# Queries and keys of heads 1 to 3 in seven block products instead of eight half-blocks

## The reference, cut to what matters

```python
def _odd_mixer(h, w_in, w_out, gammas):
    proj = h @ w_in                       # h: 512 x 1024, w_in: 1024 x 6144
    q, k, v, g = jnp.split(proj, [D_MODEL, 2 * D_MODEL, 4 * D_MODEL], axis=-1)
    o = _retention(_split_heads(q, RET_HEADS), _split_heads(k, RET_HEADS),
                   _split_heads(v, RET_HEADS), gammas)
    ...
    y = (jax.nn.silu(g.astype(jnp.float32)) * o).astype(h.dtype)
    return y @ w_out
```

## Time and profile before

| | us |
|---|---|
| median of three runs | 1286.79 (1286.78 to 1287.39) |
| the profiled execution, device time | 1287.36 |
| its span in the trace | 1285.6 |
| `r_qk(1)`, PE, from 664.75 | 21.8 |
| `r_qk(2)`, PE, from 777.24 | 21.8 |
| `r_qk(3)`, PE, from 847.99 | 21.8 |

### The profile page before, as it was taken

The page is one execution under the profiler, slowest core; times in us unless marked ns, Lnnn a source line. Parts: engine busy times, 40 slices in busy tenths (PEclk is TensorE's granted clock), DMA queues, the critical chain, the costliest instruction groups (busy, mean ns, idle before and its releaser), DMA issues.

```text
span 1285.6 us, 18945 instructions
## 1 busy us (share of the span) xinstructions
PE 1276.6 (99%) x7390; PEld 1119.9 (87%) x7390; DVE 913.6 (71%) x1171; ACT 733.5 (57%) x992; POOL 211.7 (16%) x253
## 2 busy tenths in 40 slices
PE   9999999999999999999999999999999999999998
PEld 6788888899898998989888888888889899898996
DVE  6466457578958669598754694656799876959678
ACT  6555455358557475576645552636667746457564
POOL 3121000022112211111211021111212221111211
PEclk9999999999999999999999999999999999999999
DMA  7322231469898988993854686755598899898983
GB/s 259 91 66 58 74 91 58 136 151 234 224 227 180 224 226 214 231 224 117 175 178 89 188 204 172 195 132 112 143 236 201 198 231 230 209 237 183 219 217 107
DMA packets 100409, 223.20 MB, mean 174 GB/s; under 512 B 8784, under 2 KB 25432, under 8 KB 100320
## 3 DMA queue, kind: packets, MB, share of 16 engines
q0 software_dynamic: 26912, 97.55, 39.7%
q1 hardware_dynamic: 73104, 124.11, 29.1%
q10 hardware_dynamic: 304, 0.33, 0.1%
HBM read 127.57 MB, written 2.11 MB: 101 GB/s over the span
## 4 chain that ended last, share of the span: by engine, by line
PE 90%; DVE 5%; DMA 2%; issue 1%; ACT 1%; POOL 0%; SPq 0%; POOLq 0%; DVEq 0%; ACTq 0%
PE bank L806 21%; PE bank L838 21%; PE bank L1207 12%; PE bank L1019 9%; PE bank L1124 7%; PE bank L1275 5%; PE bank L959 3%; PE bank L936 3%; PE bank L1221 2%; PE bank L986 2%; DVE w L1978 2%; PE bank L921 1%; PE bank L1173 1%; PE bank L903 1%; PE bank L901 1%
## 5 line engine op out<-in xcount | busy, mean ns | idle before, releaser
L1978 DVE TENSOR_TENSOR w<-raw_tiles,w 128x1024 fp32r<-128x1024 f32 x324 | 385.5, 1220 | 116.7 <-ACT w L1408 116.4
L1408 ACT ACTIVATE w<-raw_tiles 128x1024 fp32r<-128x1024 f32 x324 | 327.7, 1051 | 153.7 <-PE bank L838 53.7
L806 PE MATMUL bank<-h_ops,w 128*128 128x256 f32 x2688 | 325.0, 283 | 0.1
L806 PEld LDWEIGHTS bank<-h_ops,w 128*128 128x128 f32 x2688 | 323.9, 192 | 1.0 <-DVE h_ops L2210 0.3
L838 PE MATMUL bank<-w,arena_q 128*128 128x512 f32 x1332 | 305.1, 390 | 0.1
L838 PEld LDWEIGHTS bank<-w,arena_q 128*128 128x128 f32 x1332 | 249.1, 188 | 52.9 <-DVE x L2254 1.7
L2741 POOL DMA_DIRECT2D raw_tiles<-raw_tiles x176 | 152.6, 902 | 664.9 <-DVE w L1978 439.3
L1207 PE MATMUL bank<-w,h_ops 128*128 128x512 f32 x672 | 154.1, 390 | 0.0
L1207 PEld LDWEIGHTS bank<-w,h_ops 128*128 128x128 f32 x672 | 125.7, 188 | 25.7
L1124 PE MATMUL bank<-h_ops,w 128*128 128x512 f32 (+1 forms) x480 | 89.5, 347 | 0.0
L1124 PEld LDWEIGHTS bank<-h_ops,w 128*128 128x128 f32 x480 | 77.3, 189 | 11.4 <-DVE h_ops L1963 0.2
(11 more groups left out here) (190 smaller groups left out, 1425.4 us busy)
## 6 DMA issues: line engine op xcount, KB each, us to landing
raw_tiles<-raw_tiles POOLq DMA_DIRECT2D x176, 512.0 KB, 5.6
raw_tiles<-in_ffn_w_in SPq DMA_DIRECT2D x64, 512.0 KB, 5.7
raw_tiles<-in_ffn_w_out SPq DMA_DIRECT2D x64, 512.0 KB, 6.2
raw_tiles<-in_odd_w_in SPq DMA_DIRECT2D x32, 512.0 KB, 4.7
raw_tiles<-in_even_w_in SPq DMA_DIRECT2D x48, 256.0 KB, 3.2
raw_tiles<-in_odd_w_in SPq DMA_DIRECT2D x32, 256.0 KB, 5.2
raw_tiles<-in_odd_w_out SPq DMA_DIRECT2D x16, 512.0 KB, 6.1
x<-in_x SPq DMA_DIRECT2D x8, 512.0 KB, 5.7
```

Of the source, the lines that this page charges most:

```text
L806: mm = pe.matmul(bank[first + b][:, 256 * m:256 * m + 256], w_slots[use_slot(use)][:, p, k, c:c + P], h_ops[:, H_BLOCK[op], q, k, :], star ...
L1408: nc.scalar.activation(w_flat(use_slot(use), 0, half), raws[tile][:, 1024 * half:1024 * half + 1024], ACT.Copy).then_inc(m_hi, 1)
L1978: nc.vector.tensor_tensor(w_flat(use_slot(use), 1, half), raws[use_tile(key)][:, 1024 * half:1024 * half + 1024], w_flat(use_slot(use), 0, ...
```

## The change

`r_qk(h)` for h = 1, 2, 3 becomes a seven-product scheme over 2x2 blocks of 256 token columns and 256 output columns (queries are the first column block of the weights, keys the second). Head 0 stays as it is. Each product is 2 output groups x 4 contraction tiles x 3 passes = 24 matmuls of 128x256, 168 in all instead of 96 of 128x512. The A operands are those which the vg section uses already.

```diff
+QK_ORDER = ((A11, B11, "X"), (A12, B21, "Z"), (S1, T1, "Y"), (S2, T2, "X"), (S4, B22, "Y"), (S3, T3, "X"), (A22, T4, "X"))
...
             def r_qk(h):
...
+                for i, (op, value, to) in enumerate(QK_ORDER):
+                    use = USE["qk", h, i // 2]
+                    for m in range(2):
...
+                        elif i == 3:
+                            pe.wait_ge(qk_copied[0], 2 * (h - 1) + m + 1)
+                        elif i == 4:
+                            pe.wait_ge(qk_copied[1], h)
+                        elif i == 5:
+                            pe.wait_ge(qk_copied[2], 2 * (h - 1) + m + 1)
+                        else:
+                            pe.wait_ge(qk_summed, 4 * (h - 1) + 3 + m)
+                        if m == 0:
+                            pe.wait_ge(m_lo, split_count("qk", h, value, 1))
```

A weight value is 128x4x256 and two values share a slot: B11 and B21, T1 and T2, B22 and T3, T4 alone. The weight tile of 128x2048 holds query and key columns side by side, so T1 is one half of a tile's columns added to the other, in pieces of 256 columns:

```diff
+            def add_columns(n, value, half, dst, src):
...
+                pool.dma_start(to, of, accum_op=ALU.add).then_inc(t_made[value][half], 16)
...
             for h in range(RH):
...
                 if h % 2 == 0:
+                    for value in (T1, T3, T2, T4):
+                        qk_weight_sum(h + 1, value)
                     gn_inv_std(h)
                     continue
...
+                    for value in (T1, T3, T2, T4):
+                        qk_weight_sum(2, value)
```

More of the change, by code:

```diff
@@ L184, in a_slot, with product_done, split_count, qk_source @@
     return (7 * g + i) % A_SLOTS
+def product_done(key, t=1):
+    return 2 * PRODUCT_COUNT[key] + t + 1
 def use_done(use, t=1):
-    return 2 * PRODUCT_COUNT[USES[use]] + t + 1
+    kind, n, part = USES[use]
+    if kind == "qk":
+        part = QK_VALUES[min(2 * part + 1, 6)]
+    return product_done((kind, n, part), t)
+def split_count(kind, n, part, half):
+    if kind == "qk" and n:
+        i = QK_VALUES.index(part)
+        return 2 * USE[kind, n, i // 2] + (2 if i == 6 else i % 2 + 1)
+    return 2 * USE[kind, n, part] + half + 1
+def qk_source(n, part):
+    tile, cols = {B11: (0, 0), T1: (0, 0), T2: (0, 0), "B12": (0, 1), T3: (0, 1), B21: (1, 0), T4: (1, 0), B22: (1, 1)}[part]
+    return TILES["qk", n][tile], slice(256 * cols, 256 * cols + 256)
+QK_LOAD = {B11: 0, "B12": 0, B21: 1, B22: 1}
 def products_done(g, i, t=1):
@@ L565, in trunk @@
         qk_done = sem("qk_done")
+        qk_copied = [sem(f"qk_copied{n}") for n in range(3)]
+        qk_summed = sem("qk_summed")
         qk_hi = sem("qk_hi")
@@ L659, in split_done @@
             def split_done(key, half):
-                sp.wait_ge(m_lo, 2 * USE[key] + half + 1)
+                sp.wait_ge(m_lo, split_count(*key, half))
             def added_by(section, values, half):
@@ L678, in tile_free @@
                 before = SECTIONS[SECTION[kind, n] - 1]
-                if before[0] == "qk":
+                if before[0] == "qk" and before[1] and part in ("B12", B22):
+                    added_by(before, (T4,), half)
+                    split_done((*before, T3 if part == "B12" else T4), half)
+                elif before[0] == "qk":
                     scheme = SECTIONS[SECTION[kind, n] - 2]
@@ L1414, in use_hi_both, with qk_value_hi @@
                 use_hi(key, 1)
+            def qk_value_hi(n, value):
+                i = QK_VALUES.index(value)
+                use, (tile, cols) = USE["qk", n, i // 2], qk_source(n, value)
+                act.wait_ge(*used(use - W_SLOTS))
+                src = raws[tile].rearrange("p (k n) -> p k n", k=4)[:, :, cols]
+                dst = w_slots[use_slot(use)][:, 0, :, 256 * (i % 2):256 * (i % 2) + 256]
+                for half in range(2):
+                    if value in t_made:
+                        act.wait_ge(t_made[value][half], SUM_COUNT["qk", n])
+                    else:
+                        act.wait_ge(m_landed[2 * tile + half], LANDED["qk", n, QK_LOAD[value]])
+                    if value == T4:
+                        k = slice(2 * half, 2 * half + 2)
+                        nc.scalar.activation(dst[:, k], src[:, k], ACT.Copy).then_inc(m_hi, 1)
+                if value != T4:
+                    nc.scalar.activation(dst, src, ACT.Copy).then_inc(m_hi, 1)
             def w_hi(stage, i, half):
@@ L1815, in r_head @@
                 else:
+                    qk_value_hi(h + 1, B11)
                     gate_silu(h, 1)
-                    use_hi_both(("qk", h + 1, 0))
+                    qk_value_hi(h + 1, B21)
                 gate_silu(h, 2)
@@ L1854, in r_out @@
                 if p == 0:
-                    use_hi_both(("qk", 2, 0))
-                    use_hi_both(("qk", 2, 1))
+                    qk_value_hi(2, B11)
+                    qk_value_hi(2, B21)
                 else:
```

198 lines of the change are left out of this document (152 added, 46 removed).

## The result

| | before | changed |
|---|---|---|
| median, us | 1286.78 (1286.37 to 1287.39, five runs) | 1293.83 (1292.97 to 1294.56, five runs) |
| ratio | | 1.0055, interval 1.004 to 1.007 |
| profiled execution, device time, us | 1287.36 | 1293.38 |
| its span, us | 1285.6 | 1291.6 |

A forecast was written before the change was run, and what follows sets the result against it. PE, busy 99% of the span, was taken to bound the kernel. Saving -4.8, holes 2 x 1.45 (heads 1, 3) and 3.9 + 0.3 (head 2) sum to +2.3 us: 1289.1 us, range 1286.1 to 1294.3.

The forecast's parts named there:

- D: Time from a value's first adding-DMA issue until both halves are ready for ACT; taken as 5.1 us, bounds 3.6 and 7.7.
- the main case: The summed forecast with its holes on PE, given 62%, with its own range 1288 to 1291 us (D from 4.6 to 6.0).
- a granted clock under 1.00 after 786: Listed sign of a wrong forecast: PE's clock dropping below its top level after 786 us.
- chain 1: B11 split, T1's adding DMA and split, then T2's, before T2's product: 3.9 us hole in head 2, covered in heads 1 and 3.
- the clock behind it: Rival, 10%: the hole lowers PE's clock, one product's work then runs at 1.2 GHz, 2.9 us more, 1292.0 us.
- chain 2: DVE's difference before T4's product comes late: PE holes of 1.45 us in heads 1 and 3, 0.2 in head 2.
- What PE saves: In `r_qk`, 168 matmuls at 0.120 us replace 96 at 0.227: 1.60 us a head, 4.8 us in all.
- The upper bound of 7.7: Rival, 13%: adding DMAs cost by the piece, D = 7.7 us, head 2 hole 9.1, sum +7.5, 1294.3 us.
- chain 3: vg's loads, asked for later, and vg's T1 adding DMA: covered by 3 us, so no wait of PE.
- `gn_inv_std` behind T4's DMA: On POOL, its first power moves to about 667.6 us instead of 663; claimed to cost nothing.
- all waits are covered: Rival: the whole saving stays, 1282.0 us, or 1285.2 with only the T2 hole gone; 8% for faster by over 0.2%.
- B11 split 4 us sooner: In head 2, sooner than DVE's row lets it: named as one alternative to D under 3.2 us for covering T2's hole.

The follow-up runs named there:

- e4: Changed kernel with DVE's sum ahead of vg's first value and the first difference between that value's halves, all heads; 1290.72 us, ratio 1.0023 to the kernel before.
- e12: e5 with SP asking for the first loads of vg(2) only when T2 of head 2 is made; 1294.46 us, ratio 1.0051 to the kernel before.
- e6: Changed kernel with T1's adding DMA in rows of 512 columns (2 KB) instead of two of 256, adding wrong columns; 1294.24 us (one run).
- e5: Changed kernel with B11's low part of head 2 four output additions earlier on DVE; 1293.01 us, ratio 1.0042 to the kernel before.
- e7: Changed kernel with e4's DVE order in heads 1 and 3, and head 2 as before the change; 1284.45 us, ratio 0.9977 to the kernel before.

## Why the prediction came out as it did

The sign was the one held likeliest, the time lies inside the range, and the three chains were the right places to look. That the time lies inside the range is luck in part. The range's upper end, 1294.3, stood for D = 7.7, and D was 5.7 to 6.0; with that and all else as forecast the sum gives about 1290.5, and the main case's own range ended at 1291. What brought the rest was the clock, which the sum left out. One of the forecast's own signs of being wrong, "a granted clock under 1.00 after 786", came true.

The sum was too small by 4.7 us, 3.5 of them in the three `r_qk`. By its own terms, profiled execution against profiled execution, us:

| term | forecast | measured |
|---|---|---|
| seven products at 0.120 a matmul, three heads | -4.8 | -4.8 (e4: 20.16 a head unbroken) |
| chain 1: hole at T2, head 2 | +3.9 | +5.3 |
| the clock behind it (a rival, 10%) | 0, or +2.9 | +2.3 |
| chain 2: difference, heads 1 and 3 | +2.9 | +2.8 |
| chain 2 in head 2 | +0.3 | 0 |
| the rest, behind the waits of heads 1 and 3 | 0 | +0.2 |
| the three `r_qk` | +2.3 | +5.8 |

The holes are counted here as the forecast counts them, from the moment at which the product is due (8.64 us after the start for T2, 17.28 for T4) to its start: 13.98 - 8.64 = 5.34 in head 2, 18.68 - 17.28 = 1.40 in heads 1 and 3. The rows' idle times, 5.18 and 1.25, are shorter by 0.15, because a row's duration runs that much beyond 0.120 a matmul (17.43 us for 144, where 144 x 0.120 is 17.28).

- **What PE saves** was right to 0.01 us a head.
- **Chain 1 was mis-sized.** Its formula, hole = 2D - 6.3, holds: with the mean of 5.66 and 6.00 it gives 5.4, measured 5.34. The wrong step is D = 5.1, "by bytes". Taking the 2.62 us between two halves of a 512-KB DMA as the time of its data, and half of that for 256 KB, was 0.6 to 0.9 us short. In e12, with no loads in flight, the two halves take 5.66 us: the data alone need 3.2 us at the measured 165 GB/s, not 2.62. The upper bound of 7.7 was not reached, and e6 speaks against a cost by the piece as large as that rival's.
- **The clock** was given 10%, as a rival to the main case. It is no rival: it comes with the hole. It came behind all ten holes from 2.06 to 5.86 us in these traces, so it would hardly have stayed away at the forecast 3.9. The term, one product at half speed or 2.9 us, was near the measured 2.3. The Trainium skill's warning (TensorE: Matmul & The Clock Gate, HAM oscillation) agrees with this trace; giving it so low a chance because the trace before shows no hole was the error of judgement. With it in the sum the forecast would have been 1292.0.
- **Chain 2** was right: 1.40 us in each of heads 1 and 3 for 1.45, from the cause named (e4). In head 2 DVE reached the difference in time.
- **Heads 1 and 3, chain 1; chain 3; `gn_inv_std` behind T4's DMA**: no wait of PE at T2 there and none in vg, as forecast. (Where the working says that seven splits come at "more than PE's 2.88 us", it means faster than one per 2.88 us.)
- **A condition of the rival "all waits are covered" was argued wrongly.** "B11 split 4 us sooner" was named as a way to cover the hole. e5 shows that 3.2 us sooner gives nothing, since loads fill the DMA engines at that time; with the loads held (e12) the same start shortens the wait by 3.3 us. The forecast never looked at what else is in flight where T1 is issued.

Behind the odd heads one output group of the second MLP takes 39.46 us (1010.37 to 1049.83) where it took 38.62 before, 0.36 of it a wait for DVE's sum. With it the profiled executions differ by 6.6 us from `r_qk(1)` on, (1291.6 - 664.15) - (1285.6 - 664.75); up to there the changed kernel's is 0.6 us ahead. That group takes 38.2 to 39.8 us in the various kernels; whether the change causes it is not settled. The two medians differ by 7.0, these two executions by 6.0; the rest is within the interval.

## What to carry to other kernels

Before a hole is opened on a PE that has had none, count it twice: its length, and the time at half speed behind it. A chain of two dependent adding DMAs with a split between them is 14.3 us long here from T1's issue until ACT has T2 (773.77 to 788.06), and nothing but an earlier start hides it, so use the scheme where that start exists (heads 1 and 3, as in e7) and leave it where it doesn't. Where DVE has two things queued, put first the one that PE waits for (e4). Before moving a DMA earlier, look at which loads already fill the engines there; holding the loads back only helps if nothing dependent is issued when they are let go.

## What the runs showed of the hardware that was not expected

- An adding DMA issued while loads are in flight starts late. With the loads held (e12) its first packets move 1.5 to 2.2 us after the issue at 771.15; in e5, issued at 771.31, none moves before 774.4, while q1 holds 95.8% of the engines from 770 to 774, 104 to 105% from 773 on. Then both queues move together until the loads end near 776.3, and ACT starts at 780.2. The Trainium skill (DMA: Bandwidth & Descriptors, Queues, rings and completion order) has each engine alternate between its queues packet by packet. The stretch after 774.4 agrees, and so does T4 in e12, 7.7 and 10.7 us beside loads; the stretch before it doesn't, and no run shows why.
- Alone, 512 KB of adding DMAs in 1-KB pieces move at about 165 GB/s (0.33 MB from 774 to 776 in e12).
- POOL needs 1.18 us to issue an adding DMA with 1-KB rows, 0.87 with rows of 2 KB (e6) and 0.86 for the 512-KB ones.
- Holes of up to 1.99 us left the clock at 1.00, those from 2.06 us on halved it, each seen in one execution (1.25 in several). The runs do not show what decides between 1.99 and 2.06.
